# Input projection on unnormalised input in order of arrival, the norm's root at eviction, and additions set among the gates

## The reference

```python
def rmsnorm(x, w):
    xf = x.astype(jnp.float32)
    y = xf * lax.rsqrt(jnp.mean(xf * xf, axis=-1, keepdims=True) + EPS)
    return (y * w.astype(jnp.float32)).astype(x.dtype)
...
    h = rmsnorm(x, attn_norm_w[l])
    proj = h @ w_in[l]                 # 1024 -> 3072, first step of the first block
...
    act = jax.nn.gelu(jnp.einsum('thkd,td->thk', u, hc), approximate=False)
    vv = expert_v[expert_idx]          # per token 8 heads x 16 of 16384 experts
    return jnp.einsum('thk,thkd->td', gate * act, vv)
...
return rmsnorm_2(x, final_g_2)         # last step of all
```

## Time and profile before

| | us |
|---|---|
| median of 3 runs (2873.76 to 2879.39) | 2875.7 |
| the profiled execution | 2878.39 |
| its span in the trace | 2876.6 |
| PE busy, 13164 matmuls | 2734.1 (95%) |
| DVE busy | 1665.0 (58%) |
| POOL busy | 1162.3 (40%) |
| ACT busy | 832.0 (29%) |

### The profile page before, as it was taken

The page is one execution under the profiler, slowest core; times in us unless marked ns, Lnnn a source line. Parts: engine busy times, 40 slices in busy tenths (PEclk is TensorE's granted clock), DMA queues, the critical chain, the costliest instruction groups (busy, mean ns, idle before and its releaser), DMA issues.

```text
span 2876.6 us, 38501 instructions
## 1 busy us (share of the span) xinstructions
PE 2734.1 (95%) x13164; PEld 2176.3 (76%) x13164; DVE 1665.0 (58%) x3283; ACT 832.0 (29%) x1245; POOL 1162.3 (40%) x976
## 2 busy tenths in 40 slices
PE   5997999999999899899899999999999999999997
PEld 4774688878788666788787777888888888888775
DVE  5256622211898457589999774444444444444887
ACT  1135133322222355133455422222222222222111
POOL 4420355555454322443300144444444444444442
PEclk9999899999999999999999999999999999999998
DMA  4210223323232221222256754344344343443442
GB/s 139 88 45 23 66 88 97 100 95 102 81 95 93 69 85 44 85 76 88 81 220 233 255 172 131 106 126 126 109 117 130 111 124 109 124 124 109 132 128 62
DMA packets 208201, 315.46 MB, mean 110 GB/s; under 512 B 139888, under 2 KB 142320, under 8 KB 203888
## 3 DMA queue, kind: packets, MB, share of 16 engines
q1 hardware_dynamic: 63792, 233.34, 25.8%
q10 hardware_dynamic: 144320, 80.94, 10.2%
HBM read 275.45 MB, written 38.80 MB: 109 GB/s over the span
## 4 chain that ended last, share of the span: by engine, by line
PE 43%; issue 22%; DVE 19%; POOL 14%; DVEq 0%; DMA 0%; ACT 0%; ACTq 0%; POOLq 0%
POOL lo L449 14%; PE bank L1312 14%; PE bank L1313 14%; PE bank L1314 14%; DVE ohg L1238 3%; DVE bank L1265 2%; DVE oh L1234 1%; DVE oh L1235 1%; DVE WH L1267 1%; DVE pr L886 1%; DVE lo L1246 1%; DVE eq L1211 1%; DVE idx L1153 1%; DVE idx L1145 1%; DVE scb L1146 1%
## 5 line engine op out<-in xcount | busy, mean ns | idle before, releaser
L449 POOL TENSOR_TENSOR lo<-raw,hi 128x256 fp32r<-128x256 f32 (+1 forms) x972 | 1162.1, 1223 | 1676.2 <-ACT hi L475 846.8
L1312 PE MATMUL bank<-inH,hi 128*128 128x512 f32 x2240 | 895.2, 400 | 27.8 <-DVE inL L818 16.2
L1313 PE MATMUL bank<-inL,hi 128*128 128x512 f32 x2240 | 880.5, 393 | 0.0
L1314 PE MATMUL bank<-inH,lo 128*128 128x512 f32 x2240 | 880.0, 393 | 0.0
L1273 DVE TENSOR_TENSOR xT<-xT,bank 128x512 f32<-128x512 f32 x504 | 339.9, 686 | 534.7 <-PE bank L1314 534.7
L1312 PEld LDWEIGHTS bank<-inH,hi 128*128 128x128 f32 x2240 | 425.8, 190 | 131.9 <-issue 33.3
L1314 PEld LDWEIGHTS bank<-inH,lo 128*128 128x128 f32 x2240 | 425.4, 190 | 90.9
L1313 PEld LDWEIGHTS bank<-inL,hi 128*128 128x128 f32 x2240 | 426.4, 190 | 88.2 <-issue 2.2
L1312 PE MATMUL bank<-WH,hi 128*128 128x512 f32 x1024 | 409.0, 399 | 15.2 <-DVE xT L1273 15.2
L1313 PE MATMUL bank<-WL,hi 128*128 128x512 f32 x1024 | 404.7, 395 | 0.0
L1314 PE MATMUL bank<-WH,lo 128*128 128x512 f32 x1024 | 399.8, 390 | 0.0
(11 more groups left out here) (211 smaller groups left out, 2392.0 us busy)
## 6 DMA issues: line engine op xcount, KB each, us to landing
raw<-stream SPq DMA_DIRECT2D x440, 512.0 KB, 3.6
Gd<-gates ACTq DMA_DIRECT2D x32, 1024.0 KB, 7.3
gates<-stage_a ACTq DMA_DIRECT2D x16, 1024.0 KB, 4.5
gates<-stage_b ACTq DMA_DIRECT2D x16, 1024.0 KB, 4.1
tbl<-gqa ACTq DMA_DIRECT2D x8, 384.0 KB, 3.2
spilled<-res ACTq DMA_DIRECT2D x12, 256.0 KB, 4.2
A<-spilled ACTq DMA_DIRECT2D x6, 512.0 KB, 3.7
xT<-x SPq DMA_DIRECT2D x1, 2048.0 KB, 8.8
```

Source lines behind the costliest of these rows:

```text
L449: ins = pool.tensor_tensor(lo[:, r, part], raw[:, r, part], hi[:, r, part].bitcast(F32), ALU.subtract)
L1312: pe.matmul(bank, wh, xh, start=start, stop=False)
L1313: pe.matmul(bank, wh, xl, start=False, stop=False)
L1314: return pe.matmul(bank, wl, xh, start=False, stop=stop_)
```

## The change

Four parts. (1) SP now issues gains, then weight slots and quarters of x by turns, then the constants and the fourth slot. (2) The start: ScalarE squares the blocks; VectorE splits x times gain, without the root, into `inH` and `inL` (`raw_split`) and adds the squares in between (`add_square`); TensorE takes pieces of the first four tiles in the order of the table `FIRST_PARTS` (tile, first block, end block), with the sums and the spread put between pieces. The root, copied to `res`, is multiplied in when a tile is moved out of PSUM; for the last tiles, which have tokens on the partitions, it is the per-partition number `rr`, in two instructions of 256 columns. GpSimd's first four subtractions are whole ones. (3) In the expert layer the adds of pair j stand among the steps of weigh(j+1). (4) At the end ScalarE squares, VectorE adds.

```diff
+X_PARTS = 4
+FIRST_PARTS = ((0, 0, 2), (0, 2, 4), (1, 0, 4), (0, 4, 6), (1, 4, 6), (2, 0, 6), (0, 6, 8), (1, 6, 8))
...
+        sq_tile = lambda k: sq[:, 0, :] if k == 0 else sq[:, 1, :] if k % 2 else res[:, :]
...  SyncE
-            sp.dma_start(xT[:, :, :], x).then_inc(small_in, 16)
-            for r in range(RING):
-                load(r, r)
+            for r in range(AHEAD):
+                load(r, r)
+                load_x(r)
+            load_x(AHEAD)
             sp.dma_start(cs[:, :], consts).then_inc(small_in, 16)
+            load(AHEAD, AHEAD)
...  GpSimd
-            with pool.Fori(0, S_PEER // RING) as i:
+            for r in range(RING):
+                low(r, r, D)
+            with pool.Fori(1, S_PEER // RING) as i:
...  ScalarE
-            table(stage1, 0)
-            act.wait_ge(small_in, 48)
-            for n in range(AHEAD):
-                high(0, 0, n, first=True)
+            def square_tile(nth, k):
+                if k >= 3:
+                    act.wait_ge(sq_added, nth * (KD - 2) + k - 2)
+                act.activation(sq_tile(k), xT[:, k, :], ACT.Square).then_inc(squared, 1)
+            act.wait_ge(gains_in, 16)
+            for p in range(X_PARTS):
+                if p < AHEAD:
+                    high(0, 0, p, first=True)
+                act.wait_ge(x_in[p], 16)
+                square_tile(0, 2 * p)
+                square_tile(0, 2 * p + 1)
+            high(S_IN, 0, AHEAD, first=True)
             root_of(TT, 1.0 / D, KD)
+            table(stage1, 0)
...
+            for k in range(KD):
+                act.wait_ge(y_added, (N_PAIRS - 1) * KD + k + 1)
+                square_tile(1, k)
             root_of(TT, 1.0 / D, n_sums + KD)
...  VectorE
+            def raw_split(gname, k):
+                chain(dve.tensor_scalar(inH[:, k, :], xT[:, k, :], gain(gname, k), None, ALU.mult))
+                dve.scalar_tensor_tensor(inL[:, k, :], xT[:, k, :], gain(gname, k), inH[:, k, :].bitcast(F32),
+                                         ALU.mult, ALU.subtract).then_inc(in_part, 1)
...
+            for k in range(KD):
+                dve.wait_ge(x_in[k * X_PARTS // KD], 16)
+                raw_split("attn", k)
+                if k >= 2:
+                    add_square(0, k - 1)
+            add_square(0, KD - 1)
...
-                    take(m, dve.tensor_scalar(qk1[:, m, :], bank[:, :], QSCALE if m < 2 else 1.0, None, ALU.mult))
+                    take(m, dve.scalar_tensor_tensor(qk1[:, m, :], bank[:, :], QSCALE, res[:, :], ALU.mult, ALU.mult))
...
+            def weigh_and_add(j0, slot, c):
+                last = j0 + (c - 1)
+                weigh(j0, slot, c, 0)
+                add(last, 0)
+                add(last, 1)
+                gated(j0, slot, c, 1)
+                add(last, 2)
+                high_part(c, 1)
+                add(last, 3)
+                low_part(c, 1)
+                for k in range(4, KD):
+                    add(last, k)
...
-                dve.wait_ge(y_added, (N_PAIRS - 1) * KD + k + 1)
-                square(x_of(k), k)
+                if k >= 2:
+                    add_square(1, k - 1)
+            add_square(1, KD - 1)
...  TensorE
-            full_norm(n_sq, n_rt)
+            for m, k0, k1 in FIRST_PARTS:
+                first_part(m, k0, k1)
+            pe.wait_ge(small_in, 16)
+            square_sums(n_sq)
+            first_part(2, 6, 8)
+            first_part(3, 0, 4)
+            pe.wait_ge(recips, n_rt)
+            spread_roots()
+            first_part(3, 4, 8)
-            first_tiles(S_IN, T_IN, 0)
```

More of the change, by code:

```diff
@@ L306, in program @@
         evac = sem("evac")
+        gains_in = sem("gains_in")
+        x_in = [sem(f"x_in{p}") for p in range(X_PARTS)]
         small_in = sem("small_in")
@@ L535, in attention @@
                         act.activation(st["dst"][:, w["dst"], :], B[2 + w["group"] % 2][:, :], ACT.Copy).then_inc(s["head_out"], 1)
-            table(stage1, 0)
-            act.wait_ge(small_in, 48)
-            for n in range(AHEAD):
-                high(0, 0, n, first=True)
+            def square_tile(nth, k):
[10 more added lines that the diff above has]
+            high(S_IN, 0, AHEAD, first=True)
             root_of(TT, 1.0 / D, KD)
             n_sums = KD
-            for r in range(RING):
-                high(S_IN, 0, r + AHEAD, first=r + AHEAD < RING)
+            table(stage1, 0)
+            for r in range(1, RING):
+                high(S_IN, 0, r + AHEAD)
             for m in range(RING, N_IN):
@@ L909, in _, with add_square @@
             x_of = lambda k: xT[:, k, :]
-            dve.wait_ge(small_in, 48)
-            n_sums, n_root, n_spread = 0, 0, 0
+            def add_square(nth, k):
+                dve.wait_ge(squared, nth * KD + k + 1)
+                if k >= 2:
+                    dve.wait_ge(sq_added, nth * (KD - 2) + k - 1)
+                ins = dve.tensor_tensor(sq_tile(0), sq_tile(0), sq_tile(k), ALU.add)
+                if k < KD - 1:
+                    ins.then_inc(sq_added, 1)
+                else:
+                    ins.then_inc(squares, KD)
+            n_sums, n_root, n_spread = 0, 0, 0
+            dve.wait_ge(gains_in, 16)
+            for k in range(KD):
[4 more added lines that the diff above has]
+            add_square(0, KD - 1)
+            dve.wait_ge(small_in, 16)
             chain(dve.tensor_copy(triR[:, :], tri))
             chain(dve.tensor_copy(onesR[:, :], ones))
-            for k in range(KD):
-                square(x_of(k), k)
-            norm(x_of, "attn", n_root + 1, n_spread)
+            root_to_sbuf(n_root + 1, n_spread)
             n_spread += 1
@@ L1254, in _, with gated @@
             assert u == BUILT
-            def weigh(j0, slot, c):
+            def gated(j0, slot, c, e):
                 buf, wpar, j = c // 2, c % 2, j0 + c
                 dve.wait_ge(g_loaded[buf], j0 * 4 + 16)
[L1260 to L1278, removed]
+                dve.wait_ge(gelu_done, j * 2 + (e + 1))
+                a = A[:, bass.ds(slot + e, 1), :].rearrange("p a (b t) -> p (a b) t", t=SPILL)
@@ new lines, in gated, with high_part, low_part, weigh @@
+                chain(dve.tensor_tensor(B[4 + e][:, :].rearrange("p (b t) -> p b t", t=SPILL), a, Gd[:, buf, :, 2 * wpar + e, :], ALU.mult))
+            def high_part(c, e):
+                chain(dve.tensor_scalar(WH[:, c % 2, e, :], B[4 + e][:, :], 1.0, None, ALU.mult))
+            def low_part(c, e):
+                dve.tensor_tensor(WL[:, c % 2, e, :], B[4 + e][:, :], WH[:, c % 2, e, :].bitcast(F32), ALU.subtract).then_inc(w_done, 1)
+            def weigh(j0, slot, c, e):
+                gated(j0, slot, c, e)
+                high_part(c, e)
+                low_part(c, e)
@@ new lines, in add @@
+            def add(j, k):
+                dve.wait_ge(y_done, j * KD + (k + 1))
+                dve.tensor_tensor(xT[:, k, :], xT[:, k, :], B[k % 4][:, :], ALU.add).then_inc(y_added, 1)
+            def weigh_and_add(j0, slot, c):
[10 more added lines that the diff above has]
+                    add(last, k)
@@ L1280, in four @@
+            weigh(0, 0, 0, 0)
+            weigh(0, 0, 0, 1)
+            for c in range(1, 4):
+                weigh_and_add(0, 2 * c, c)
             def four(j, slot):
                 for c in range(4):
-                    weigh(j, slot + 2 * c, c)
-                    adds(j + (c - 1))
+                    weigh_and_add(j, slot + 2 * c, c)
             steps = 4 * 2 * 2
```

43 lines of the change are left out of this document (32 added, 11 removed).

## The result

The changed kernel takes 2837.0 us (median of 4 runs, 2831.7 to 2839.7); the kernel before takes 2874.8 in the same comparison (4 runs, 2873.8 to 2879.4). The ratio is 0.986, 95% interval 0.9847 to 0.9872: faster by 1.3 to 1.5%, some 38 us.

What follows compares the result with a forecast made beforehand. TensorE was taken as the bound in the middle, so gains come where it stands still: 15.5 (start) + 19.5 (loop) + 6.1 (end) - 0.2 (evictions) = 40.9, from the median 2834.8 us; range 2828 less 1 to 2847.

Steps and rivals of the forecast that it cites:

- The start: First projection's first four tiles: TensorE begins sooner, tile 3 ends at 41.3 us instead of 56.75, gaining 15.5 us.
- the copy: Start: ScalarE's copy behind tile 3, at 56.80 us before, marks the tile's end, forecast seen at 41.3.
- the list: Hand-made timetables of steps at the start and in the loop, giving when each transfer, split, subtraction or add is done.
- The lower level: Start: TensorE's lower clock, a matmul every 0.43 us instead of 0.23, expected until about 16 to 20 us.
- The rival of a longer one: Start: TensorE stays at the lower clock until about 30 us, costing 6.6 us, time 2841; chance 0.13.
- Evictions: Moving tiles out of PSUM: four instructions replace two for the last two tiles; 0.2 us lost, bounds 0 and 0.7.
- The loop: Expert layer: TensorE no longer waits for VectorE's adds, twenty waits at 0.97 us each, gaining 19.5 us.
- The upper bound: Loop: gain of at most 21 us, if a mix without a wait runs at the middle stretch's 0.230.
- the second gate multiplication: Loop: VectorE step after add 1, put at 1.49 us and done 6.3 us into the mix.
- the rival in which the loop's stall moves: Loop: second multiplication against GpSimd takes longer, add 3 has 1.5 us slack; half the gain lost, 10 us; chance 0.08.
- The slower rival: Loop: new order holds TensorE in the 42 pairs with `ahead`; slower overall from 0.97 us a pair; chance 0.03.
- The end: After the last mix: last square added 4.8 us earlier, root's table load hidden for 1.28 more; gain 6.1 us.

Runs made afterwards that it cites:

- e6: Changed kernel with GpSimd's first four subtractions each cut into four pieces of 256 columns instead of whole; 2836.2 us.
- e7: Changed kernel with the first tiles one after another (tile 0, tile 1, six blocks of tile 2), not interleaved by arrival; 2842.2 us.
- e5: Changed kernel with SyncE issuing gains, constants, the four quarters of x, then the four slots; 2841.5 us.
- e12: The changed kernel run once more, unaltered; 2838.3 us, ratio 0.9865 to the kernel before.
- e2: The kernel before with only the new order of gate steps and adds in the loop; 2859.8 us.
- e9: The kernel before, leaving out only ScalarE's last wait for a mix where no copy stands behind it; 2876.9 us against 2878.3.
- e4: Changed kernel with the old end (VectorE adds, squares and adds up; table load where the compiler puts it); 2845.0 us.
- e3: Changed kernel with the old order in the loop (both gate steps, then eight adds); 2854.9 us.
- e11: Changed kernel with tile 2 ahead of the sums and 26 TensorE matmuls on ones before its first block; 2835.5 us.
- e10: Changed kernel with tile 2's blocks 0 to 3 before tile 0's block 4, and all tile 2 before the sums; 2835.5 us.

## Why the prediction held

- **The start (15.5 predicted, 15.7 to 16.7 measured** in five profiles). From block 5 on the steps met their rows: block 5 split at 22.97 (23.05), last split at 26.55 (26.85), sums at 32.01 (32.05), spread at 36.99 (37.5), the copy 0.4 earlier than 41.3. Those 0.4 to 0.5 are the sums and the spread: each holds the row of matmuls up by 0.8 (31.78 to 32.82 in place of 0.23), 1.6 for both, where 2.1 was taken. Ahead of block 5 the list was off: slot 0 and the first quarter of x came at 5.63 and 7.63 instead of 5.0 and 6.1 (at 4.9 and 6.9 at best in other profiles), the second subtraction followed the first at once, and block 1 was split at 14.24, not at 10.95. It cost little, since blocks 4 and 5, behind the third subtraction, come at their times all the same, and from there TensorE hardly waits. That VectorE stands still beside GpSimd was right; a whole subtraction took it 2.0 to 2.2 us (2.6 taken). The lower level lasted until 17 to 20 us, in the range given (16 to 20). The rival of a longer one did not come in the changed kernel; it did come in e6 (until 21.8) and in e7 (again until 28.6).
- **The gain of the start comes from order as well as from the root.** The prediction didn't split it. e5 and e7 do in part: arrival order is 6.2 us, the order of pieces 5.8, each taken away alone and read in one profile. What moving the root alone brings was not tested, nor the squares on ScalarE or the whole subtractions against before.
- **Evictions (0.2 lost).** The four instructions of the last pair of tiles take 1.66 us where two took 1.29, but the lead behind them is what it was (15.72 and 15.76 in e12 at the copy and at the head of the loop). The term is nothing at this place.
- **The loop (19.5 predicted, 19.1 measured).** Twenty waits at 0.95 instead of 0.97. The price from the period was right and the drawn idle time, 15.2, was too low by a fifth. The upper bound doesn't follow from its reason: 48 matmuls at 0.230 are 11.04, and 20 x (12.17 - 11.04) is 22.6, not 21. No mix ran at 0.230: the pair took 11.20 as the block's 1.40 said. The list's one wrong entry is the second gate multiplication, 2.64 and not 1.49: behind two adds it starts just when GpSimd starts. That is the rival in which the loop's stall moves; its mechanism came in part, its slack shrank from 1.5 to 0.9, and it did not reach TensorE.
- **The 42 pairs with `ahead`** gained and lost nothing: e2 is 4.44 us ahead at the first matmul of the seventh mix (1744.47 before, 1740.03) and 4.44 ahead at that of the forty-ninth (2661.76). The slower rival needed 0.97 a pair.
- **The end (6.1 predicted, 6.1 measured** in both profiles of the changed kernel). 1.4 for the load (e9), the rest for the squares; with the part undone 0 (e4). In e3 it is 7.0 and in e7 7.8, because TensorE was faster there: the sums took 1.05 us in both, 1.86 in the first profile, and in e7 the spread took 1.16 instead of 2.08. That it came to them at its upper level is likely, but the rows don't show the level there.

## What to carry to other kernels

Price a wait from the period of the stretch with it and without it, not from the drawn gap: here 0.95 against 0.76 us a wait. When a projection waits for a norm, the root can go to the eviction, but the time also comes from letting parts of both operands arrive by turns and from taking pieces across tiles: undoing either order gave back 6 us of 16, for the pieces in part because TensorE, working with gaps, stayed at its lower clock for longer. And before a difference between two profiles is explained, look at stretches that the change doesn't touch: here they carried 5.6 us, and the same start differed by 1 us between profiles.

## What was not expected of the hardware

- A granted clock of 0.97 or 1.00 in the same stretch of the same kernel, from one execution to the next, worth 1.5 us in 50.
- TensorE can fall back to a spacing of 0.43 in the midst of a start that had reached 0.23: in e7 it did so after only three matmuls between 18.1 and 22.7 us.
- The column of the granted clock doesn't show the lower level at the start in each profile. In the changed kernel's stretch with a spacing of 0.43 it says 1.00, in e11's 0.51:

```profile
11.00:18.20 7.20, 5.48 (x11) 3.39 (x12) 7.09 (x9) 1.87 (x3) 2.65 (x2) 1.00 0.85 345
```

```profile
14.00:20.00 6.00, 6.00 (x14) 4.25 (x15) 5.89 (x9) 2.21 (x3) 1.73 (x1) 0.51 0.62 252
```

  There the spacing of matmul starts has to be read.
- One instruction of VectorE that starts within a whole subtraction of GpSimd ends 0.3 to 0.6 us after it, wherever it starts: 2.57 to 2.81 us long beside one from its beginning, 1.88 in e10, where it starts 0.75 later, and the same for a gate multiplication from A and Gd that alone is 0.69.

```profile
7.61 2.35 POOL L462 TENSOR_TENSOR lo<-raw,hi 128x1024 fp32r<-128x1024 f32 x1 [7.16 <-ACT hi L490]
8.36 1.88 DVE L853 TENSOR_SCALAR inH<-xT,gn 128x512 fp32r<-128x512 f32 x1 [8.36 <-DMA xT<-x]
```
